# Three product units for two in each gate/up chunk, their column sums made in place in eight raw weight buffers, one of the sums by an adding transfer from GpSimd

## What is computed

```python
h = h + 0.5 * swiglu(rms_norm(h, ffn1_norm[l]), ffn1_w_gate[l], ffn1_w_up[l], ffn1_w_down[l])
...
def swiglu(x, w_gate, w_up, w_down):
    return (jax.nn.silu(x @ w_gate) * (x @ w_up)) @ w_down
```

## Time and profile before

| | |
|---|---|
| median of 3 runs | 1834.85 us (1834.80 to 1835.28) |
| span of the profiled execution, first to last instruction | 1834.2 us (its own time is recorded as this span alone; 0.65 us less than the median) |
| PE, PEld busy | 99%, 84% of the span |
| DVE, ACT, POOL busy | 82%, 54%, 1% |
| granted clock of PE | 0.999 |
| 16 groups of a gate/up chunk | 42.16 us |

### The profile page before, as it was taken

The page is one execution under the profiler, slowest core; times in us unless marked ns, Lnnn a source line. Parts: engine busy times, 40 slices in busy tenths (PEclk is TensorE's granted clock), DMA queues, the critical chain, the costliest instruction groups (busy, mean ns, idle before and its releaser), DMA issues. The chain is left out here.

```text
span 1834.2 us, 29749 instructions
## 1 busy us (share of the span) xinstructions
PE 1819.6 (99%) x10696; PEld 1546.4 (84%) x10696; DVE 1505.4 (82%) x1755; ACT 995.2 (54%) x1181; POOL 11.1 (1%) x23
## 2 busy tenths in 40 slices
PE   9999999999999999999999999999999999999998
PEld 7888888888888888999998878888888888888886
DVE  5888888888988985788867866688888888889996
ACT  7555555545555655754535655545555555555554
POOL 1000000000000000000000000000000000000000
PEclk9999999999999999999999999999999999999999
DMA  7677666777766778564443557677777677676664
GB/s 252 221 219 228 219 216 215 220 229 236 233 202 204 225 224 267 173 184 140 138 116 106 176 171 261 180 232 231 229 224 232 216 227 222 217 240 195 209 208 157
DMA packets 207851, 380.36 MB, mean 207 GB/s; under 512 B 16016, under 2 KB 35728, under 8 KB 207504
## 3 DMA queue, kind: packets, MB, share of 16 engines
q1 hardware_dynamic: 206768, 377.08, 65.7%
q10 hardware_dynamic: 480, 1.97, 0.3%
q0 software_dynamic: 512, 0.06, 0.0%
HBM read 360.19 MB, written 18.87 MB: 207 GB/s over the span
## 5 line engine op out<-in xcount | busy, mean ns | idle before, releaser
L402 ACT CAST whi<-raw 128x1024 fp32r<-128x1024 f32 (+1 forms) x648 | 675.1, 1047 | 700.8 <-DVE raw L1476 189.6
L411 DVE TENSOR_TENSOR wlo<-raw,whi 128x1024 fp32r<-128x1024 f32 (+1 forms) x648 | 771.7, 1212 | 208.4 <-ACT whi L402 194.5
L428 PE MATMUL psA<-whi,xh 128*128 128x512 f32 (+1 forms) x572 | 219.5, 384 | 0.5 <-DVE wlo L411 0.5
L428 PE MATMUL psA<-whi,xl 128*128 128x512 f32 (+1 forms) x572 | 219.2, 383 | 0.0
L428 PE MATMUL psA<-wlo,xh 128*128 128x512 f32 (+1 forms) x572 | 219.1, 383 | 0.0
L428 PE MATMUL psB<-whi,xh 128*128 128x512 f32 x544 | 211.7, 389 | 0.0
L428 PE MATMUL psB<-wlo,xh 128*128 128x512 f32 x544 | 211.6, 389 | 0.0
L428 PE MATMUL psB<-whi,xl 128*128 128x512 f32 x544 | 211.6, 389 | 0.0
L428 PEld LDWEIGHTS psA<-whi,xh 128*128 128x128 f32 x572 | 107.4, 188 | 21.6 <-DVE wlo L411 0.7
L428 PEld LDWEIGHTS psA<-whi,xl 128*128 128x128 f32 x572 | 107.4, 188 | 21.2
L428 PEld LDWEIGHTS psA<-wlo,xh 128*128 128x128 f32 x572 | 107.4, 188 | 21.0
(11 more groups left out here) (520 smaller groups left out, 3447.3 us busy)
## 6 DMA issues: line engine op xcount, KB each, us to landing
raw<-in_ffn_w_gate SPq DMA_DIRECT2D x176, 512.0 KB, 4.5
raw<-in_ffn_w_up SPq DMA_DIRECT2D x176, 512.0 KB, 4.6
raw<-in_ffn_w_down SPq DMA_DIRECT2D x176, 512.0 KB, 4.6
raw<-in_w_in SPq DMA_DIRECT2D x80, 512.0 KB, 3.6
raw<-in_w_out SPq DMA_DIRECT2D x32, 512.0 KB, 4.2
quads_dram<-stage SPq DMA_DIRECT2D x88, 128.0 KB, 4.2
stage<-quads_dram SPq DMA_DIRECT2D x22, 512.0 KB, 4.3
x<-in_x SPq DMA_DIRECT2D x4, 512.0 KB, 7.5
```

Source lines behind the costliest of these rows:

```text
L402: nc.scalar.copy(whi[:, slot, :, 0:ncol], raw[:, slot, :, 0:ncol]).then_inc(hi_ready, 1)
L411: nc.vector.tensor_tensor(wlo[:, slot, :, 0:ncol], raw[:, slot, :, 0:ncol], whi[:, slot, :, 0:ncol].bitcast(F32), ALU.subtract).then_inc(l ...
L428: mm = nc.tensor.matmul(ps[:, tb, 0:ncol], lhs[:, k0 + t, tok], rhs[:, slot, t, 0:ncol], start=(first and t == 0 and p == 0 and tb != open ...
```

## The change

Three units for two: `CHUNK` now has units at g4/g5, g8/g9 and g12/g13 and ten plain groups. What else it does:

- `raw` gets four more buffers for these chunks (`deep0`, `deep1`, in the part of the arena that holds the network's inner result of the last two chunks), so a load waits for the group eight places before it. For a unit's buffers it waits for `col_lo`, since
- the column sums are made in the raw buffers themselves, after both groups are split (`column_sums`, three adds), and `col_hi` and `col_lo` are made one item of `CHUNK` later (`columns_hi`, `columns_lo`);
- a fourth sum, that of the two row blocks of the up group, is made before the splits by a transfer: GpSimd loads the second block once more and adds it to the first in the buffer (`add_up`, 256 KB). ACT and DVE wait for it (`wait_up`);
- the close of a chunk is put into the next chunk: ACT copies `Q1` and applies silu after its split of g1, DVE closes after its split of g1, and `turned_*` moves from behind g1 (ACT: from the chunk's end) to behind g2. silu's two halves are counted apart, and PE's first group waits for each half when it comes to it (`second_half`);
- the transposed result is stored at g14 and loaded in the next chunk at g1; the token sums cover three pairs of blocks, and some semaphores elsewhere are shared to make room.

```diff
-GATE_UNITS = 2
+GATE_UNITS = 3
 GATE_PAIR = 2
-CHUNK = ([("gate", j) for j in (0, 1, 4, 5)] + [("unit", 0)] + [("gate", j) for j in (6, 7)] + [("up", 0)] + [("unit", 1)]
-         + [("up", j) for j in (1, 4, 5, 6, 7)])
+CHUNK = ([("gate", j) for j in (0, 1, 5, 6)] + [("unit", 0), ("gate", 7), ("up", 0), ("unit", 1), ("up", 1), ("up", 5), ("unit", 2)]
+         + [("up", j) for j in (6, 7)])
+DEEP = 8
...
+        def wait_split(sp, f, n, j):
+
+            unit = unit_of(f, j)
+            if unit is not None:
+                sp.wait_ge(col_lo_ready, n * GATE_UNITS + (unit + 1))
+            else:
+                sp.wait_ge(hi_ready, n * PER + (base_of[f] + j + 1))
+                sp.wait_ge(lo_ready, n * PER + (base_of[f] + j + 1))
...
+        def add_up(pool, f, base, n, j, g, w):
+
+            wait_raw(pool, base, n, PER, g + 1)
+            if not (isinstance(n, int) and f == 0 and j == 0):
+                pool.wait_ge(up_summed, n * (16 * GATE_UNITS) + 16 * (GATE_TOTAL * f - GATE_UNITS + j))
+            pair = GATE_PAIR + j
+            second = w[(pair * KT + 1) * P:(pair * KT + 2) * P, :]
+            pool.dma_start(raw_pair(g % DEEP)[:, 2, :], second[:, bass.ds(n * COLS, COLS)], accum_op=ALU.add)\
+                .then_inc(up_summed, 16)
+
+        def column_sums(f, base, n, j, g):
+
+            V = nc.vector
+            two = raw_pair(g % DEEP)
+            steps = n * (COL_STEPS * GATE_UNITS)
+            V.wait_ge(lo_ready, n * PER + (base + g + 2))
+            tt(two[:, 2, :], two[:, 0, :], two[:, 2, :], ALU.add).then_inc(col_step, 1)
+            V.wait_ge(col_step, steps + (first_col(f, j) + 1))
+            tt(two[:, 1, :], two[:, 2, :], two[:, 1, :], ALU.add).then_inc(col_step, 1)
+            tt(two[:, 0, :], two[:, 2, :], two[:, 3, :], ALU.subtract).then_inc(col_step, 1)
...
             def chunk(n):
+                begun = None
                 for kind, j, g in chunk_items():
                     split_hi(base, n, PER, g)
+                    if begun:
+                        columns_hi(f, n, *begun)
+                        begun = None
+                    if g == 1 and not (isinstance(n, int) and n == 1):
+                        copy_share(n - 1)
+                        silu_gate(n - 1)
+                    if g == 2 and not (isinstance(n, int) and n == 1):
+                        turned_hi(n - 2)
                     if kind == "unit":
...
+                        wait_up(nc.scalar, f, n, j)
                         split_hi(base, n, PER, g + 1)
...
+                        begun = j, g
...
             def chunk(n):
+                begun = None
                 for kind, j, g in chunk_items():
                     if kind == "unit":
...
+                        wait_up(nc.vector, f, n, j)
+                    split_lo(base, n, PER, g)
+                    if kind == "unit":
                         split_lo(base, n, PER, g + 1)
...
+                        column_sums(f, base, n, j, g)
+                    if begun:
+                        columns_lo(f, n, *begun)
+                        if begun[0] == 0:
                             turn_quads(n - 1)
...
+                        begun = None
+                    if kind == "unit":
+                        begun = j, g
                     if g == 1 and not (isinstance(n, int) and n == 1):
+                        close_gate(n - 1)
+                    if g == 2 and not (isinstance(n, int) and n == 1):
                         turned_lo(n - 2)
...
                     if g == SLOTS - 1:
                         gate_up(n - 1)
-                    if g == PER - 2:
-                        close_gate(n)
```

More of the change, by code:

```diff
@@ L377, in build @@
         substituted = sem("substituted")
-        def load_group(sp, src, base, n, per, j, ncol=COLS):
[L383 to L394, removed]
+        base_of = (0, FC * PER + DC * GF + MIX_GROUPS)
@@ new lines, in is_deep, with raw_slot, raw_of, raw_pair @@
+        def is_deep(n, per):
+            return per > 0 and not (isinstance(n, int) and n == 0)
+        def raw_slot(base, n, per, j):
+            return j % DEEP if is_deep(n, per) else (base + j) % SLOTS
+        def raw_of(slot):
+            return raw[:, slot, :, :] if slot < SLOTS else deep[slot // 2 - 2][:, slot % 2, :, :]
+        def raw_pair(slot):
+            two = raw[:, slot:slot + 2, :, :] if slot < SLOTS else deep[slot // 2 - 2][:, :, :, :]
+            return two.rearrange("p s t c -> p (s t) c")
@@ L416, in wait_group, with project_tokens @@
             nc.tensor.wait_ge(lo_ready, n * per + base + j + 1)
[L419 removed]
+        def project_tokens(ps, h, l, base, n, per, j, k0, first, last, ncol=COLS, between=None, open_half=None, second_half=None):
             wait_group(base, n, per, j)
@@ L431, in project_tokens, with unit_products @@
             mm.then_inc(group_used, 1)
-        def unit_products(base, n, per, g, whole, pair, sums, j, unit, first, last):
+        def unit_products(base, n, per, g, whole, pair, sums, j, unit, first, last, order=(0, 1, 2)):
             gate, up = (base + g) % SLOTS, (base + g + 1) % SLOTS
@@ L451, in column_sums @@
             def column_sums(k):
-                return [arr[:, k, :] for arr in (col_hi, col_lo)]
+                return [arr[:, order[k], :] for arr in (col_hi, col_lo)]
             wait_group(base, n, per, g)
@@ L658, in ffn_load, with first_chunk @@
         def ffn_load(sp, f, base, w_gate, w_up, w_down):
[L659 to L670, removed]
+            def first_chunk():
                 for j in range(SLOTS if f == 0 else 0, GD):
@@ L810, in sum_number, with unit_lo @@
+        def unit_lo(unit):
+            nc.vector.wait_ge(unit_used, unit)
+            nc.vector.wait_ge(col_hi_ready, unit + 1)
+            tt(col_lo[:, :, :], col_raw[:, :, :], col_hi[:, :, :].bitcast(F32), ALU.subtract).then_inc(col_lo_ready, 1)
         def sum_number(f, b=None):
@@ L1017, in ffn_dve, with ffn_pool, chunk @@
                 gain_dve(2)
+        def ffn_pool(pool, f, base, w_up):
+            def chunk(n):
+                for kind, j, g in chunk_items():
+                    if kind == "unit":
+                        add_up(pool, f, base, n, j, g, w_up)
+            chunk(1)
+            with pool.Fori(2, FC) as n:
+                chunk(n)
         def add_down(f, down, c):
@@ L1452, in build @@
         count = {}
+        counted = {f"{name}{n}": (name, n + 1) for name in ("exp", "recip") for n in range(4)}
         def done(ins, name):
-            if name in steps:
+            if name in counted:
+                ins.then_inc(steps[counted[name][0]], 1)
+            elif name in steps:
                 ins.then_inc(steps[name], 1)
```

230 lines of the change are left out of this document (156 added, 74 removed), and 2 rows, old and new, of the table steps.

## The result

The changed kernel takes 1845.39 us (median of 4 runs, 1844.41 to 1848.95) against 1834.91 for the kernel before: **0.58% slower**, ratio 1.0058, 95% interval 1.0044 to 1.0073. Forecast were 1829.2 us and a gain. The profiled execution took 1845.3 us and spans 1843.5, 9.3 more than before.

What follows compares the result with a forecast made beforehand. The prediction took PE's matrix products to bound the gate/up chunks. Fewer products gain 13.6 us, waits cost 7.6 in looped chunks and 0.4 in chunk 1, leaving 5.6: 1829.2 us, range 1822 to 1846.

Steps and rivals of the forecast that it cites:

- PE bounds the kernel: Gate/up chunks: PE never idles; 183 products for 186 cut a chunk from 42.16 to 41.48 us, 13.6 over 20 chunks.
- The chain to the first unit's `col_lo`: Looped chunks, ACT and DVE from last unit's end: `col_lo` at 19.29, due 18.77; 0.42 us lost each, 7.6 in all.
- The floor of 0.18: First unit of every chunk: sums after both splits, then `col_hi`, `col_lo`, lose 0.18 us however free DVE is.
- The second unit holds by 0.1: Second unit of a chunk: next `col_lo` begins at 10.13 us, PE needs 10.2, so no wait.
- The add: 5.6 us, limit 6.5: GpSimd's adding transfer, tightest at the third unit: takes 5.6 us, may take 6.5, so it costs nothing.
- Chunk 1 has no close before it: First unit of chunk 1, both networks: shorter chain, `col_lo` 0.28 us late, 0.18 lost, twice: 0.4.
- the first unit's add has three us more: Adding transfer of a chunk's first unit: three us more room than the third unit's, so no cost.
- the eight buffers: Raw load buffers of these chunks: costed at nothing, since PE had no waits that a load could end.
- the token sums: Token sums, wider by half: costed at nothing, some 0.1 us per network.
- The one on a late add: Looped chunks' third unit: each us over 6.5 costs one per looped chunk; 1847 us at 7.5; chance 0.25.
- Its second way: POOL's issue waits for a DVE instruction, up to 1.75 us: add 7.4, time 1845; 0.06 of the 0.25 chance.
- The sum: Whole kernel: 13.6 - 7.6 - 0.4 = 5.6 us gained; span 1828.6, time 1829.2, with 0.65 between them.

Runs made afterwards that it cites:

- g1_order: Changed kernel with chunk 1's loads into empty buffers first, the transposed result's reload behind the down product's first load, and `turned_hi`/`turned_lo` ahead of waits: 1824.96 us, ratio 0.9940.
- f3: Changed kernel with chunk 1's loads into empty buffers first, later reload of the transposed result, and all 60 up-group sums made by DVE: 1853.93 us, ratio 1.0095.
- e1: Changed kernel with only chunk 1's loads of g4 to g7, into empty buffers, issued ahead of those of g0 to g3: 1832.99 us, ratio 0.9981.
- f1: Changed kernel with chunk 1's loads into empty buffers first, later reload of the transposed result, and `turned_lo` moved from DVE to GpSimd: 1831.09 us, ratio 0.9972.
- e4: Changed kernel with GpSimd's 60 adding transfers replaced by plain loads, so the up groups' sum is left out: 1840.07 us, ratio 1.0024.

## Why the prediction was wrong

- *PE bounds the kernel; 183 products take 41.48 us.* Right; g1_order shows the chunk.
- *The chain to the first unit's `col_lo`, 0.52 late, 0.42 lost per looped chunk.* Right in mechanism and place, the size nearly: 0.25 lost. The rows of the looped chunk that begins at 230.59, in the changed kernel: PE's first product after the last unit, DVE's `col_lo`, and the weight load that waits for it.

```profile
225.15 0.39 PE L502 MATMUL psB<-whi,xh 128*128 128x512 f32 x1
...
242.48 1.76 DVE L1640 TENSOR_TENSOR col_lo<-deep,col_hi 128x1536 fp32r<-128x1536 f32 x1 [0.49 <-ACT col_hi L912]
...
244.29 0.19 PEld L513 LDWEIGHTS psM<-col_hi,x_sum_hi 128*128 128x128 f32 x1 [0.36 <-DVE col_lo L1640]
```

  `col_lo` ended 19.09 us after the unit (244.24), against 19.29 worked out. The loss in the loop was 6.5 us (18 chunks against 41.48), forecast 7.6. Of it 4.5 are the common wait at the first unit. The other 2 belong to some chunks alone: some 1.3 at third units, with adds of 5.6 to 6.3 us, and 0.7 at the first unit of the chunk behind three of them.
- *The floor of 0.18 "for the other chunks too", "however free DVE is".* Wrong: g1_order's looped chunks are 41.48 to 41.51 mostly, so with a shorter chain nothing of it is left.
- *The second unit holds by 0.1.* Right: no wait in the loop, and 0.33 to 0.45 us of one as soon as DVE had 0.69 more to do (f3).
- *The add: 5.6 us, limit 6.5, the third unit the one that matters.* Half right. In the changed kernel it takes 3.9 to 4.8 us in second units, with one or two loads beside it, 6.3 to 7.5 in first units, among some six transfers, and 4.3 to 7.8 in third ones. The 4.6 us for a load was not the row for an add among seven queued loads. The limit was tighter than 6.5: an add of 7.2 us made PE wait 1.9 in the last chunk of e1, so 5.2 was allowed there (6.0 in the second network); POOL could start only 25.8 us after the unit, not 24.6.
- **The step that failed: "Chunk 1 has no close before it. There the chain is shorter ... 0.18 lost, twice: 0.4."** Two chunks of 41.66 us were forecast, and 48.55 and 50.15 measured: 15.4 us of the 16.2 between 1829.2 and 1845.4. The chain was counted from PE, ACT and DVE alone, as if the add of the first unit were there; "the first unit's add has three us more" is true of the loop, where its loads are issued a chunk ahead, and nowhere else. What stood behind it were two costs that I had put at nothing: the eight buffers ("PE had no waits that a load could end"), though SP's queue at the change from four buffers to eight puts the loads for empty buffers behind those for full ones; and the token sums ("some 0.1 per network"), whose later place held up a split by 1.9 us, and with it the queue. The late add then made PE wait 1.7 and 3.6 us in the first network, and the half clock behind that, which had no term either, cost 1.6 more there and 2.9 in the second. Once the add is early, little is left of it: 0.47 and 0.62 us are lost in e1, where 0.18 was forecast. That rest is DVE's, as the rows of e1's first network show:

```profile
62.72 2.35 DVE L483 TENSOR_TENSOR wlo<-deep,whi 128x1024 fp32r<-128x1024 f32 x2
...
68.68 1.76 DVE L1643 TENSOR_TENSOR col_lo<-deep,col_hi 128x1536 fp32r<-128x1536 f32 x1 [0.42 <-ACT col_hi L915]
```

  DVE works without a break from g0's split on, with the rest of the token sums (1.7 us) in between. It ends the split of g5 8.50 us after the chunk's start (56.57), not 8.10, and `col_lo` 13.87 after it, not 13.61.
- *The rivals.* The one on a late add had the mechanism, with the third unit of every looped chunk as its place and 1845 or 1847 us as prices; the measured 1845.4 is the same number from another place. That it lies inside the range of 1822 to 1846 is luck, then. Its second way, GpSimd held up by DVE, shows nowhere: POOL's issues take 0.86 to 0.90 us in all rows, beside a DVE at work.
- *The sum.* It was made with 0.65 us around the span. Every later run shows 1.7 to 1.9 between its own time and its span, and so makes some 1.2 of the 16.2 us; before's profiled execution has no time of its own, so how much of this was wrong before stays open. (The stretch ahead of the first chunk 1 adds 0.7, and the loop gives 1.1 back.)

The Trainium skill ("DMA: Bandwidth & Descriptors", section on issuing engines that are not separate DMA queues) says that transfers of SP and GpSimd run on the same 16 engines and interleave. That fits the runs: an add took 4.2 us with little company and 7.0 among six transfers. By the formula of the same page, weighed in the prediction, it would be 2.6, an estimate that no add here comes near.

## What to carry to other kernels

A change to a loop has to be followed through the iteration ahead of the loop as well: which transfers are queued behind which there, and who waits for the last one. Where the number of buffers grows on the way, loads into buffers that are still empty belong ahead of loads that wait. A transfer on the path has to be priced with what runs beside it at that moment, not by its row on an idle queue.

## What was not expected of the hardware

- PE at half clock after waits: behind the one of 3.6 us in chunk 1, 7 products ran at 1.2 GHz in the first network and 13 in the second (3.7 us), which cost 1.6 and 2.9 us on top. With the waits gone the mean granted clock is 0.999 (e1) for 0.996.
- In f1 a split on DVE took 1.67 in place of 1.22 us beside a subtraction on GpSimd (1.51 to 1.70 in all 18 looped chunks), and the add into PSUM right behind it its usual 1.22. The Trainium skill ("SBUF — State Buffer", section on who interferes with whom) has a DVE instruction with two SBUF inputs contend with a GpSimd instruction that reads SBUF, and the trace agrees, with 0.45 us. The two subtractions of 128x512 take 3.52 us on GpSimd and 1.28 on DVE.
- POOL's issue of an adding transfer keeps it 0.86 to 0.90 us, that of the plain one 0.54 (2.17 for four, in e4's chunk 1).
